# A queue of sixteen 1 MB weight blocks, down products in 64-row tiles with the tokens as columns, and 88 token slots

## The reference, cut to what matters

```python
def moe_swiglu(h, router_w, w_gate, w_up, w_down):
    xt = h.reshape(B * T, D)
    logits = (xt @ router_w).astype(jnp.float32)
    top_val, top_idx = lax.top_k(logits, TOP_K)
    gates = jax.nn.softmax(top_val, axis=-1)
    combine = jnp.einsum("nk,nke->ne", gates, jax.nn.one_hot(top_idx, N_EXPERTS, dtype=jnp.float32))
    y = jnp.zeros((B * T, D), dtype=jnp.float32)
    for e in range(N_EXPERTS):
        y = y + combine[:, e:e + 1] * swiglu(xt, w_gate[e], w_up[e], w_down[e])
```

## Time and profile before

| | |
|---|---|
| median of 3 runs | 1775.73 us (1773.81 to 1777.84) |
| the profiled execution: its time | 1774.55 us |
| its span, first to last instruction | 1772.7 us |
| mean granted TensorE clock, share of full speed | 0.983 |
| DMA: moved, mean rate over the span | 432.65 MB, 244 GB/s |
| expert weights | 336 DMAs of 1 MB (1.0486 MB each) |

### The profile page before, as it was taken

The page is one execution under the profiler, slowest core; times in us unless marked ns, Lnnn a source line. Parts: engine busy times, 40 slices in busy tenths (PEclk is TensorE's granted clock), DMA queues, the critical chain, the costliest instruction groups (busy, mean ns, idle before and its releaser), DMA issues.

```text
span 1772.7 us, 41606 instructions
## 1 busy us (share of the span) xinstructions
PE 1706.9 (96%) x19036; PEld 1253.6 (71%) x19036; DVE 281.9 (16%) x553; ACT 197.6 (11%) x462; POOL 144.0 (8%) x164
## 2 busy tenths in 40 slices
PE   7999999999999987999999998999998999999997
PEld 6787577777778746777777775777776777777774
DVE  3433400001434342001001001001001001001002
ACT  3133210000313222000000000000000000000000
POOL 2243200000225221000000000000000000000000
PEclk9999999999999987999999998999998999999999
DMA  9202354443421333998998996998998899899892
GB/s 332 96 18 104 127 181 143 143 142 132 155 96 48 123 119 133 347 350 308 351 349 303 351 352 224 343 350 307 351 348 301 280 349 352 303 351 354 299 352 98
DMA packets 311448, 432.65 MB, mean 244 GB/s; under 512 B 9050, under 2 KB 263260, under 8 KB 311276
## 3 DMA queue, kind: packets, MB, share of 16 engines
q1 hardware_dynamic: 310396, 427.75, 70.1%
q0 software_dynamic: 672, 2.14, 0.4%
q10 hardware_dynamic: 208, 0.08, 0.0%
HBM read 428.90 MB, written 1.05 MB: 243 GB/s over the span
## 4 chain that ended last, share of the span: by engine, by line
PE 93%; DVE 2%; ACT 1%; issue 1%; POOL 1%; SPq 0%; DMA 0%; DVEq 0%
PE ps L856 35%; PE ps L869 23%; PE ps L759 8%; PE ps L488 7%; PE ps L770 3%; PE ps L637 3%; PE ps L499 3%; PE ps L881 2%; PE ps L623 1%; PE ps L608 1%; PE ps L834 1%; PE ps L619 1%; PE ps L514 1%; PE ps L521 1%; PE ps L629 1%
## 5 line engine op out<-in xcount | busy, mean ns | idle before, releaser
L856 PEld LDWEIGHTS ps<-bv_sb,ring 128*64 128x64 f32 x14336 | 601.2, 138 | 102.0 <-issue 102.0
L856 PE MATMUL ps<-bv_sb,ring 128*64 128x96 f32 x14336 | 622.5, 248 | 15.1 <-issue 14.5
L869 PE MATMUL ps<-ring,LT_sb 128*96 128x512 f32 x896 | 410.9, 601 | 0.0
L869 PEld LDWEIGHTS ps<-ring,LT_sb 128*96 128x96 f32 x896 | 137.0, 163 | 191.6 <-issue 179.3
L1513 DVE TENSOR_TENSOR LT_sb<-LT_sb,ps 128x192 f32<-128x192 f32 x112 | 39.6, 354 | 929.2 <-ACT LT_sb L1140 929.2
L759 PE MATMUL ps<-hT_sb,ring 128*128 128x256 f32 (+1 forms) x768 | 155.7, 362 | 0.0
L759 PEld LDWEIGHTS ps<-hT_sb,ring 128*128 128x128 f32 x768 | 136.0, 190 | 24.6 <-issue 9.1
L1140 ACT ACTIVATE LT_sb<-ps 128x192 f32<-128x192 f32 x112 | 37.1, 331 | 961.2 <-PE ps L856 961.2
L488 PE MATMUL ps<-hT_sb,ring 128*128 128x256 f32 x608 | 136.3, 382 | 0.0
L488 PEld LDWEIGHTS ps<-hT_sb,ring 128*128 128x128 f32 x608 | 115.1, 192 | 16.1 <-issue 0.5
L1564 POOL TENSOR_SCALAR small<-small 128x1 f32<-128x1 f32 x16 | 4.1, 255 | 1360.1 <-ACT XT_sb L959 1334.2
(11 more groups left out here) (259 smaller groups left out, 966.6 us busy)
## 6 DMA issues: line engine op xcount, KB each, us to landing
ring<-in_moe_w_gate SPq DMA_DIRECT2D x112, 1024.0 KB, 6.0
ring<-in_moe_w_up SPq DMA_DIRECT2D x112, 1024.0 KB, 8.9
ring<-in_moe_w_down SPq DMA_DIRECT2D x112, 1024.0 KB, 10.8
ring<-in_ffn_w_gate SPq DMA_DIRECT2D x11, 1024.0 KB, 5.2
ring<-in_ffn_w_up SPq DMA_DIRECT2D x11, 1024.0 KB, 7.8
ring<-in_ffn_w_down SPq DMA_DIRECT2D x11, 1024.0 KB, 9.7
ring<-in_w_in SPq DMA_DIRECT2D x14, 768.0 KB, 6.5
ring<-in_w_out SPq DMA_DIRECT2D x8, 768.0 KB, 5.5
```

The source lines that it names most:

```text
L856: ins = mm(o[lo:lo + P // 2, :], w[:, k, i * P + lo:i * P + lo + P // 2], xgT[:, k, :], start=(k == 0), stop=(k == KD - 1))
L869: ins = mm(bank(2 + half)[0:SLOTS, :], moe_hid[c % 2][:, i, :], d[:, i, half * 512:(half + 1) * 512], start=(c == 0 and i == 0), stop=(c = ...
```

## The change

- **Slots.** 88 token slots instead of 96, with the round limits 88 and 176. Every product with tokens as columns gets 88 of them.
- **Units.** The ring becomes, for the experts, a queue of N_UNIT = 16 units of 1 MB, each one matrix part (g, u or d) of a chunk, with a semaphore of its own. Twelve lie in the old ring, and four in a new tile `late` (32 KB in each partition), whose space mixer 1 uses for wT01, wT45, qk, bv, kend, sbk, Vn, sbz and sbp until it is done. The order is that of PE's use: g0 u0 g1 u1 d0 g2 u2 d1 and so on, at an expert's end d12 d13. PE releases each unit by itself (`unit_used`), and waits for each by itself. Units 0 to 5 wait for the same releases as before, 6 to 9 for `dno_ps` and `sb_ss`, 10 to 15 for the end of mixer 1's output product.
- **Down products.** 32 products with 64-column weights of w_down and the hidden [128, 88] moving, as in gate and up; the result is y transposed, [D, slots], in banks 2 and 3. ACT and DVE copy it to `yT`, PE transposes it back (8 transposes, into banks 4 and 5, after the next expert's first gate and up product), ACT and DVE copy again to y_tok, and the scatter follows behind the next expert's chunk 1 (gate and up) and chunk 0 (down). DVE's accumulation stands behind its chunk 1.
- **No loop over pairs.** All eight experts are written out on PE, ACT, DVE and SP; the loop over rounds stays. ACT's silu waits for the release of the chunk's up unit.
- **Places.** xgT moves to wpost, the sum to h_sb, the third part of h to XT_sb; the memset of the sum comes after the rests of h on POOL, and DVE waits for it ahead of the first accumulation instead of ahead of the stage.

The diff, cut to its core (ACT's and DVE's expert loops follow PE's):

```diff
-PAIRS = N_EXP // 2
 FF_E = 3584
 EPS = 1e-6
-SLOTS = 96
+SLOTS = 88
 ROUND_LIMITS = (SLOTS, 2 * SLOTS)
...
+UNIT = 2048
+N_OWN = NSLOT * SLOT // UNIT
+N_UNIT = N_OWN + 4
+UNITS = {}
+for _e in range(N_EXP):
+    for _c in range(MOE_CH):
+        UNITS["g", _e, _c] = len(UNITS)
+        UNITS["u", _e, _c] = len(UNITS)
+        if _c:
+            UNITS["d", _e, _c - 1] = len(UNITS)
+    UNITS["d", _e, MOE_CH - 1] = len(UNITS)
+ROUND_UNITS = len(UNITS)
+assert ROUND_UNITS % N_UNIT == 0
...
-        wT01 = sb("wT01", 2 * 3 * P)
-        wT45 = sb("wT45", 2 * 3 * P)
+        late = sb("late", (N_UNIT - N_OWN) * UNIT + 512)
+        late_at = [0]
+
+        def early(cols):
+            late_at[0] += cols
+            return late[:, late_at[0] - cols:late_at[0]]
+
+        wT01, wT45 = early(2 * 3 * P), early(2 * 3 * P)
         wpost = sb("wpost", D)
-        qk_sb = sb("qk_sb", DN_H * 2 * T)
-        bv_sb = sb("bv_sb", NPR * P)
-        kend_sb = sb("kend_sb", DN_H * P)
+        qk_sb, bv_sb, kend_sb = early(DN_H * 2 * T), early(NPR * P), early(DN_H * P)
...
+        yT = v3(hT_sb, KD, 0, KD * SLOTS)
...
+        def unit_of(n):
+
+            i = n % N_UNIT
+            if i < 3:
+                return ring[:, 3 * SLOT + i * UNIT:3 * SLOT + (i + 1) * UNIT]
+            if i < 6:
+                return ring[:, (i - 3) * UNIT:(i - 2) * UNIT]
+            if i < 10:
+                return late[:, (i - 6) * UNIT:(i - 5) * UNIT]
+            return ring[:, SLOT + (i - 10) * UNIT:SLOT + (i - 9) * UNIT]
+
+        def gate_unit(n):
+            return unit_of(n).rearrange("p (k f) -> p k f", k=KD)
+
+        def down_unit(n):
+            return unit_of(n).rearrange("p (i d) -> p i d", i=FC // P)
+
+        def per_round(r, n, a_round):
+            return r * a_round + n
...
-            def moe_pair(pair, it):
-                for j in range(2):
-                    for c in range(MOE_CH):
-                        n = FIRST_MOE + j * MOE_CH + c
-
-                        sp_.wait_ge(ring_used, it * (2 * MOE_CH) + (n - NSLOT + 1))
-                        f = slice(c * FC, (c + 1) * FC)
-                        e = pair * 2 + j
-                        load_ffn(n, moe_gate[0, e][:, f], moe_up[0, e][:, f], moe_down[0, e][f, :])
-
-            with sp_.Fori(0, PAIRS) as pair:
-                moe_pair(pair, pair)
+            def first_free(n):
+
+                if n < 6:
+                    sp_.wait_ge(ring_used, FIRST_MOE - NSLOT + 1 + n // 3)
+                elif n == 6:
+                    sp_.wait_ge(dno_ps, DEPTH)
+                    sp_.wait_ge(sb_ss, DEPTH * TT)
+                elif n >= 10:
+                    sp_.wait_ge(ring_used, FIRST_MOE - 1 + (n - 10) // 3)
+
+            def moe_loads(r, first):
+                for (kind, e, c), n in UNITS.items():
+                    if first and n < N_UNIT:
+                        first_free(n)
+                    else:
+                        sp_.wait_ge(unit_used, per_round(r, n - N_UNIT + 1, ROUND_UNITS))
+                    f = slice(c * FC, (c + 1) * FC)
+                    if kind == "d":
+                        dst, src = down_unit(n), moe_down[0, e][f, :].rearrange("(i p) d -> p i d", p=P)
+                    else:
+                        dst = gate_unit(n)
+                        src = (moe_gate if kind == "g" else moe_up)[0, e][:, f].rearrange("(k p) f -> p k f", p=P)
+                    sp_.dma_start(dst, src).then_inc(unit_landed[n % N_UNIT], 16)
+
+            moe_loads(0, True)
...
+            def landed(r, n):
+                pe.wait_ge(unit_landed[n % N_UNIT], per_round(r, 16 * (n // N_UNIT + 1), 16 * ROUND_UNITS // N_UNIT))
+
+            def m_gate_up(r, e, c):
                 if c == 0:
-                    pe.wait_ge(xg_ready, it * 4 + 2 * (j + 1))
+                    pe.wait_ge(xg_ready, per_round(r, 2 * (e + 1), 2 * N_EXP))
                 if c >= 2:
-                    pe.wait_ge(mhid_ready, it * (2 * MOE_CH) + (j * MOE_CH + c - 1))
-                g, u, _ = gate_up_down(n)
-                for i in range(FC // P):
-                    for which, w in enumerate((g, u)):
+                    pe.wait_ge(mhid_ready, per_round(r, MOE_CH * e + c - 1, MOE_CH * N_EXP))
+                for which, kind in enumerate("gu"):
+                    n = UNITS[kind, e, c]
+                    landed(r, n)
+                    w = gate_unit(n)
+                    for i in range(FC // P):
                         o = bank(c % 2)[:, (2 * which + i) * SLOTS:(2 * which + i + 1) * SLOTS]
                         for k in range(KD):
                             for lo in (0, P // 2):
                                 ins = mm(o[lo:lo + P // 2, :], w[:, k, i * P + lo:i * P + lo + P // 2], xgT[:, k, :],
                                          start=(k == 0), stop=(k == KD - 1))
-                ins.then_inc(mgu_ps, 1)
-
-            def m_down(it, j, c, tail=False):
-
-                d = gate_up_down(FIRST_MOE + j * MOE_CH + c)[2]
-                pe.wait_ge(mhid_ready, it * (2 * MOE_CH) + (j * MOE_CH + c + 1))
-                if tail and c == 0:
-                    pe.wait_ge(y_act, it * 2 + j)
-                    pe.wait_ge(y_dve, it * 2 + j)
+                    ins.then_inc(unit_used, 1)
+
+            def m_down(r, e, c):
+
+                n = UNITS["d", e, c]
+                landed(r, n)
+                pe.wait_ge(mhid_ready, per_round(r, MOE_CH * e + c + 1, MOE_CH * N_EXP))
+                if e and c == 0:
+                    pe.wait_ge(yT_act, per_round(r, e, N_EXP))
+                    pe.wait_ge(yT_dve, per_round(r, e, N_EXP))
+                d = down_unit(n)
                 for i in range(FC // P):
-                    for half in range(2):
-                        ins = mm(bank(2 + half)[0:SLOTS, :], moe_hid[c % 2][:, i, :],
-                                 d[:, i, half * 512:(half + 1) * 512],
-                                 start=(c == 0 and i == 0), stop=(c == MOE_CH - 1 and i == 1))
-                ins.then_inc(ring_used, 1)
-
-            def scatter(it, j):
-
-                pe.wait_ge(ohT_ready, it * 2 + (j + 1))
-                pe.wait_ge(y_act, it * 2 + (j + 1))
-                pe.wait_ge(y_dve, it * 2 + (j + 1))
+                    for m in range(KD):
+                        o = bank(2 + m // 4)[:, m % 4 * SLOTS:(m % 4 + 1) * SLOTS]
+                        for lo in (0, P // 2):
+                            ins = mm(o[lo:lo + P // 2, :], d[:, i, m * P + lo:m * P + lo + P // 2], moe_hid[c % 2][:, i, :],
+                                     start=(c == 0 and i == 0 and m % 4 == 0), stop=(c == MOE_CH - 1 and i == 1),
+                                     skip_group_check=True)
+                ins.then_inc(unit_used, 1)
+
+            def y_transposes(r, e):
+
+                pe.wait_ge(yT_act, per_round(r, e + 1, N_EXP))
+                pe.wait_ge(yT_dve, per_round(r, e + 1, N_EXP))
+                for m in range(KD):
+                    ins = nc.tensor.transpose(bank(4 + m // 4)[0:SLOTS, m % 4 * P:(m % 4 + 1) * P], yT[:, m, :], ident)
+                ins.then_inc(yT_ps, 1)
+
+            def scatter(r, e):
+
+                pe.wait_ge(ohT_ready, per_round(r, e + 1, N_EXP))
+                pe.wait_ge(y_act, per_round(r, e + 1, N_EXP))
+                pe.wait_ge(y_dve, per_round(r, e + 1, N_EXP))
                 for t in range(TT):
                     for half in range(2):
-                        ins = mm(bank((6, 4)[t] + half), onehotT[j][:, t * P:(t + 1) * P],
+                        ins = mm(bank((6, 4)[t] + half), onehotT[e % 2][:, t * P:(t + 1) * P],
                                  y_tok[:, half * 512:(half + 1) * 512], start=True, stop=True)
                     ins.then_inc(scatter_ps, 1)
 
-            def expert(it, j, tail, nxt):
-
-                for c in range(MOE_CH):
-                    m_gate_up(it, j, c)
-                    if c:
-                        m_down(it, j, c - 1, tail)
-                    if tail and c == 0:
-                        scatter(*tail)
-                if nxt:
-                    if tail:
-                        for t in range(TT):
-                            pe.wait_ge(moe_acc[t], it * 2 + j)
-                    gather(*nxt)
-                m_down(it, j, MOE_CH - 1)
+            def accumulated(r, e):
+                for t in range(TT):
+                    pe.wait_ge(moe_acc[t], per_round(r, e + 1, N_EXP))
 
             pe.wait_ge(part_ready, 3 * TT)
             pe.wait_ge(ident_ready, 1)
             with pe.Fori(0, rounds) as r:
-                first = r * PAIRS
-                gather(first, 0)
-                expert(first, 0, None, (first, 1))
-                with pe.Fori(0, PAIRS - 1) as pair:
-                    it = r * PAIRS + pair
-                    expert(it, 1, (it, 0), (it + 1, 0))
-                    expert(it + 1, 0, (it, 1), (it + 1, 1))
-                last = r * PAIRS + (PAIRS - 1)
```

(101 more changed lines are left out.)

96 lines of the change are left out of this document (51 added, 45 removed).

## The result

The changed kernel takes 1717.38 us (median of four runs, 1712.81 to 1724.32) where the kernel before takes 1775.56 us: ratio 0.9674 (95% interval 0.9646 to 0.9702). It is faster, as predicted, but by 58 us and not by 148, and it lies outside the predicted range. The profiled execution took 1712.81 us, with a span of 1710.9 us and a mean granted clock of 0.988.

A forecast was written before the change was run, and what follows sets the result against it. PE bound the stage before by only 6%; afterwards the DMA ends it: 687.9 + 912 + 2.9 = 1602.8 us, against PE's 1578. The end gives span 1622.3, profiled 1624.1; with clock and median allowances, forecast 1628, range 1600 to 1668.

The forecast's parts named there:

- rival (e): Expert stage, instruction supply: a missed block costs 3.6 us; 50 missed of some 172 bring back the old time; 1.5%.
- PE's part: Expert stage on TensorE: shorter products, no jump stalls (14.5 us); PE alone would end at 1578 us.
- 3 us on the DMA's side: Expert stage, DMA engines: some 48 more instruction blocks over 16 engines add 3 us of traffic.
- the rate under 355: Sign of being wrong: DMA rate stays under 355 GB/s, where 365 to 372 was expected from 700 to 1600 us.
- 1.48 us a chunk: Expert stage on PE: gate, up and down products of a chunk take 7.55 us, 1.48 less than before.
- the weight-loading rival (a): PE's narrow products: loading weights limits them to 42.4 ns at 88 columns, total 1666 us; 6%.
- The DMA's part: Expert weights after the first 16 units: 335.5 MB at 369 GB/s from 687.9 us, ending the stage at 1602.8.
- rival (b): Expert weight loads: the 369 GB/s do not last; 348 gives 1683 us, 340 gives 1706; 11% for 361 and less.
- its lead: Expert stage: PE uses up 16 waiting units at about 1270 us, then keeps step, losing about 0.19 us a unit.
- rival (d): From 1270 us PE waits at every unit; lower clock held gives 1910 us; sustained 2%, partly, up to 1668, 3%.
- The deep queue: Expert weight queue: 16 MB instead of 12, released by unit, ends the DMA's dips; remaining weights take 909 us.
- The end: After the last unit lands: down 2.5 us, then 14.95 as before, plus copy 0.7, transposes 1.2, hand-over 0.1.

The follow-up runs named there:

- half_contraction: The changed kernel with half of the gate and up products left out and all weights loaded; one run, 1642.38 us.
- old_down: The changed kernel with the down products of before (512 columns) and no y transposes; 1703.45 us, ratio 0.9586 to the kernel before.
- half_tiled: The changed kernel with down products narrow for bank 2 and 512 columns wide for bank 3, alternating per block; 1696.38 us, ratio 0.9543.
- narrow_first: half_tiled with all 32 narrow down records of a chunk first, then the four of 512 columns; 1677.34 us, ratio 0.9421.

## Why the prediction was wrong

**The step that failed** is rival (e): "Straight-line code at 272 instructions in 9 us missed none; 384 in 8.6 is unproven. 1.5%", and with it the sentence in PE's part by which writing the experts out takes the stalls away. Stalls at jumps did go (14.5 us). But the change also raised PE's demand for instructions, from 272 in 9.03 us to 384 in 7.28, a block per 4.85 us instead of one per 8.5. A fetch beside a full weight queue takes 5.9 to 6.6 us. 120 blocks were late, by 142.6 / 120 = 1.2 us each, where (e) had 3.6 a block and 50 of them for the whole gain: more often, and more cheaply. A block missed at a jump is fetched from nothing (in the kernel before PE stops at 1078.07, the packet starts at 1078.84 and PE goes on at 1081.62), while a late block in straight-line code has been on its way since about when the block before it began, so the price of one at a jump was the wrong row for it. In the sum itself PE's share of this term was nothing: more blocks were counted only as traffic, 3 us on the DMA's side. The warning could be had from the rows: of the pair of stalls the first ends at 1081.62 and the second at 1087.61, so the second block came 6.0 us after the first, and the new code eats one in 4.85. The rivals that were given weight were PE's time per record, the DMA's rate and the clock.

So it was PE with its waits for code that ended the stage, not the DMA. Of the signs of being wrong that the prediction names, one came true, the rate under 355 (347 over 700 to 1600 us), but not for the reason that it stood for: half_contraction draws 364 from the same loads. That the change is faster all the same is not owed to the step that was to bring most of it. Of the forecast's 1.48 us a chunk, 1.08 were the narrow down products, and the kernel without them is 14 us faster than the one with them.

**PE's products: right, sized 0.27 us too high a chunk.** 37.9 ns a record against 39.3 in runs of narrow products; the weight-loading rival (a) fell. The y transposes took 1.06 us for 1.2, the scatter 3.63 as said.

**The DMA's part: right in kind, not reached.** The prefetch ran as described; the first release came at 685.73 for 687.9. half_contraction shows the floor 14 us later than the forecast had it, at 364 GB/s, between the 369 taken and the 361 where rival (b) begins. By it the kernel can't end before about 1640, and the change stopped 75 us above that. One reading in this part does not follow from its own terms: 25 us lost at 0.19 us a unit are some 130 units, so that PE would have used up its lead near 1230 and not 1270. The forecast time does not hang on it; the 1910 of rival (d) would be almost 40 us more.

**The deep queue: priced as the cure for the DMA's dips, but the dips were not what held PE.** PE waited for no weight before, and waits for none now. SP's waits for room (866 us) say that loads were always ready to go.

**The clock in lock-step (d): not tested in the changed kernel, and seen in part in half_contraction.** The changed kernel waits for no unit, and its granted clock is 1.00 from 700 to 1600. In half_contraction, where PE waits for nearly every unit, the clock fell 31 times but came back each time, 130 of 807 us at the lower level. The Trainium skill (TensorE: Matmul & The Clock Gate, HAM oscillation) describes such a clock that falls at DMA waits in every step; this trace agrees that it falls, at waits of at most 2.8 us, though not in every step. The only place where it shows in the time is the very end, where the last 128 records took 6.74 us and the full change has 4.88. With all its products PE would have had far less time to spare, so what (d) would have cost stays open.

**The end: right.** From the last down product to the end 1710.9 - 1694.16 = 16.7 us, for 17.0.

**Where the 58 us come from**, each median against the runs of the kernel before beside it. The slots alone bring 53 us; old_down brings 74, so the units and the written-out experts are worth 21, of them 13 the jump stalls; the other 8 were not taken apart. The narrow down products take 16 back. By the profiled spans that last part closes: without stalls the narrow form would save 1701.9 - 1568.3 = 134 us over old_down (148 of shorter products less the transposes and hand-overs of y), and the stalls cost 143. The 9 us left are the difference of the two spans; that of the medians is 14.

What stays open: what the instruction packet waits for in the 3.4 us before it starts. Weight packets ahead of it in the same 16 engines are the likely reason, and a slow memory the less likely one, since the packet itself takes 1.09 us with a full load of weights and with a quarter of it. But the order of packets inside an engine was not looked at, and a version with fewer bytes in flight at the same rate was not tried.

## What to carry to other kernels

Count the instructions per microsecond of a stage beside its bytes: with the weights filling the DMA engines, straight-line code was free here at a block of 256 per 8.1 us (old_down), nearly free at one per 6.6 (half_tiled, 2.6 us), and beyond that cost what a block fell short of about 6 us. A cut of work that is made of many small instructions can then bring less than a smaller cut in large ones, as here; mixing both forms, sorted so that they change once each way per chunk, gave the best of both (1677 us). When both of two near bounds predict a large gain, ask for the third resource that the change uses more of, and price it at its demand after the change.

## What the runs showed of the hardware

- Instruction blocks: one per 4.85 us is sustained with no stall at a DMA share of 0.36 and nearly none at 0.93 (4.9 us); at 1.01 one takes 5.9 us (the full change) and at 1.07 up to 6.6 us (half_contraction). The packet itself takes 1.1 us in all of them, and PE goes on 1.2 to 1.6 us after it has landed.
- float32 products with 64-column weights take 37.9 ns a record at 88 columns and 5.28 us / 128 = 41.3 ns at 96; a switch to 512-column products costs 0.08 (narrow_first) to 0.12 us (half_tiled), and one back 0.15 us.
- One core's weight loads in runs of 1 and 4 KB hold 364 GB/s for 880 us.
- At waits for the DMA of at most 2.8 us, PE's granted clock fell to the lower level 31 times in 807 us (half_contraction).
